# Page table in one transfer with the third weight block held back, and the samples' tile first in both output projections, in four column tiles

## What is computed

```python
def reference(x_prompt, x_sample, cache_kv_cmp, ..., page_table, w_in_even, ..., w_out_even, w_in_odd, ..., w_out_odd, ln_g, ln_b):
    for layer in range(DEPTH):                       # DEPTH = 2
        if layer % 2 == 0:                           # projection, convolution branch, sparse attention, output projection
            dp, a1, a2, a3, a4 = even_prompt(xp, w_in_even[j], ...)
            ds, b1, b2, b3, b4 = even_sample(xs, cache_kv_cmp[j], ..., page_table, w_in_even[j], ...)
        else:                                        # projection, pooling mixer, output projection
            dp, a5 = pool_mixer(xp, buf0, 0, w_in_odd[j], ...)
            ds, b5 = pool_mixer(xs, state_pool[j], past_len, w_in_odd[j], ...)
        ...
        xp = layer_norm(DEEPNORM_ALPHA * xp + dp, ln_g[layer], ln_b[layer])
        xs = layer_norm(DEEPNORM_ALPHA * xs + ds, ln_g[layer], ln_b[layer])
```

## Time and profile before

| | us |
|---|---|
| runs, median (lowest to highest) of 3 | 1087.09 (1086.37 to 1089.18) |
| the profiled execution, span | 1087.4 |
| PE busy | 1034.4 (95%) |
| DVE busy | 757.0 (70%) |
| ACT busy | 371.3 (34%) |
| POOL busy | 368.9 (34%) |

### The profile page before, as it was taken

How to read it: one execution, slowest core, us unless ns; L and a number is a source line. 1 busy time by engine, 2 the same in 40 slices (tenths; PEclk the granted TensorE clock), 3 DMA queues, 4 the chain that set the end, 5 groups by cost and what they waited for, 6 DMA issues and landing times.

```text
span 1087.4 us, 19270 instructions
## 1 busy us (share of the span) xinstructions
PE 1034.4 (95%) x7749; PEld 882.3 (81%) x7749; DVE 757.0 (70%) x1399; ACT 371.3 (34%) x784; POOL 368.9 (34%) x385
## 2 busy tenths in 40 slices
PE   6999999999999989989899999999999999999997
PEld 6888999999999955656555666787999999998875
DVE  3677889999899978877577755757545710267755
ACT  3211111212222657868566864201112211353000
POOL 3544530000110497866685652300122311318000
PEclk9999999999999999989999999999999999999998
DMA  8654322143312034130773058521231121042321
GB/s 239 219 169 175 116 100 59 39 178 102 113 40 44 1 112 134 40 118 2 229 239 117 2 203 223 156 83 63 78 97 39 39 58 46 1 155 78 136 82 63
DMA packets 85889, 113.75 MB, mean 105 GB/s; under 512 B 21952, under 2 KB 67144, under 8 KB 85727
## 3 DMA queue, kind: packets, MB, share of 16 engines
q1 hardware_dynamic: 71849, 69.51, 21.4%
q0 software_dynamic: 11776, 41.95, 11.5%
q10 hardware_dynamic: 2182, 1.16, 0.4%
HBM read 100.91 MB, written 16.64 MB: 108 GB/s over the span
## 4 chain that ended last, share of the span: by engine, by line
PE 78%; DVE 8%; DMA 4%; issue 3%; POOL 3%; ACT 2%; another core or an unknown queue 1%; SPq 1%; DVEq 0%; POOLq 0%; ACTq 0%
PE PS L786 23%; PE PS L2200 16%; PE PS L1968 13%; PE PS L1295 5%; PE PS L1425 5%; PE PS L1313 4%; PE PS L768 3%; PE PS L1992 2%; DMA WRAW<-in_w_in_even 2%; PE PS L1981 1%; DMA WOR<-in_w_out_even 1%; DVE ACC L608 1%; PE PS L2180 1%; DVE PT L1483 1%
## 5 line engine op out<-in xcount | busy, mean ns | idle before, releaser
L655 DVE SCALAR_TENSOR_TENSOR Y<-U,SM,Y 128x1024 f32<-128x1024 f32 x120 | 150.2, 1313 | 0.4
L786 PE MATMUL PS<-XH,WH 128*128 128x352 f32 x600 | 136.3, 331 | 0.0
L786 PE MATMUL PS<-XL,WH 128*128 128x352 f32 x600 | 133.7, 327 | 0.0
L786 PE MATMUL PS<-XH,WL 128*128 128x352 f32 x600 | 132.8, 325 | 0.0
L2307 POOL TENSOR_TENSOR WL<-WRAW,WH 128x1024 fp32r<-128x1024 f32 x14 | 37.5, 2675 | 208.7 <-ACT WH L2252 208.7
L608 DVE SCALAR_TENSOR_TENSOR ACC<-PS,SM,ACC 128x508 f32<-128x508 f32 x124 | 86.9, 742 | 25.1 <-PE PS L768 21.7
L786 PEld LDWEIGHTS PS<-XH,WH 128*128 128x128 f32 x600 | 101.2, 189 | 1.2
L786 PEld LDWEIGHTS PS<-XH,WL 128*128 128x128 f32 x600 | 101.6, 189 | 0.0
L786 PEld LDWEIGHTS PS<-XL,WH 128*128 128x128 f32 x600 | 101.4, 189 | 0.0
L2200 PE MATMUL PS<-XH,WH 128*128 128x352 f32 x360 | 77.2, 323 | 0.0
L2200 PE MATMUL PS<-XH,WL 128*128 128x352 f32 x360 | 77.1, 323 | 0.0
(11 more groups left out here) (364 smaller groups left out, 2009.6 us busy)
## 6 DMA issues: line engine op xcount, KB each, us to landing
WRAW<-in_w_in_even SPq DMA_DIRECT2D x16, 512.0 KB
WRAW<-in_w_in_odd SPq DMA_DIRECT2D x16, 512.0 KB, 4.0
TM<-in_state_win_kv SPq DMA_DIRECT2D x12, 512.0 KB
XIN<-in_x_prompt SPq DMA_DIRECT2D x8, 512.0 KB, 13.6
WRAW<-in_w_in_even SPq DMA_DIRECT2D x16, 256.0 KB
XR<-in_x_prompt SPq DMA_DIRECT2D x8, 512.0 KB, 3.6
layer_out<-R SPq DMA_DIRECT2D x8, 512.0 KB, 2.7
XR<-layer_out SPq DMA_DIRECT2D x8, 512.0 KB, 3.4
```

The lines of the kernel that those rows point to most:

```text
L655: v.scalar_tensor_tensor(dst, src, CWT[:, i, t:t + 1], dst, ALU.mult, ALU.add).then_inc(s_cv, 1)
L786: ins = pe.matmul(PS[0:mcols, 3 * slot + c, 0:CH], w[:, slot, kk, 0:mcols], x[:, kk, c * CH:(c + 1) * CH], start=(kk == 0 and n == 0), sto ...
```

## The change

In words, first at the start of the kernel:

- POOL loads the page table by one transfer, 8 rows of 16 numbers. DVE copies it eight times over into PTX, PE turns that into 128 partitions, and DVE makes the row numbers behind four tiles' low parts instead of six. PE's small transposes wait for these numbers.
- SP waits until weight block 1 has landed before it issues block 2.
- POOL makes the low part of block 0 in two halves, with a semaphore each. PE runs the first four weight rows behind tile 3, and tile 4 after them.

Then in both output projections:

- `TILES` begins with the samples' tile. The first parts are those of positions 1, 2 and 3; the samples' tile follows, then the rest. Banks, semaphore counts and, in layer 0, the points at which finished tiles are turned move with it.
- The samples' tile is computed in plain fp32 from the raw weights, with XS = XH + XL made by DVE: four weight blocks at a time in four column tiles, so that four partial sums lie in four groups of 32 partitions. DVE adds them.
- In layer 0 all eight raw blocks have a buffer of their own. SP loads blocks 6 and 7 directly behind 4 and 5, then the first two blocks of layer 1, and only behind the samples' matmuls GB and the pool state. ACT converts those two blocks of layer 1 after the first two square roots.

```diff
@@ sp_program @@
             sp.dma_start(STC[:, :, :], state_conv[0].rearrange("(a b) t c -> (b t) a c", a=2)).then_inc(s_stc, 16)
+            sp.wait_ge(s_raw[1], raw_need[1])
             for m in range(2, NM + 1):
@@ pool_program @@
-            for r in range(8):
-                po.dma_start(idx[r::8, 0:8], page_table.rearrange("b n -> n b")).then_inc(s_pt, 16)
+            po.dma_start(idx[0:DB, 0:NPG], page_table).then_inc(s_pt, 16)
...
-            low(po, 0)
-            po.wait_ge(s_idx, 1)
+            po.wait_ge(s_wh, 1)
+            for kks, sem in ((slice(0, 4), s_const), (slice(4, KT), s_wl)):
+                po.tensor_tensor(WL[:, 0, kks, :], WRAW[:, 0, kks, :], WH[:, 0, kks, :].bitcast(F32), ALU.subtract)\
+                    .then_inc(sem, 1)
+            po.wait_ge(s_idx, 3)
@@ dve_program @@
-            for tt in range(6):
+            v.wait_ge(s_pt, 16)
+            v.tensor_copy(PTX[:, :].rearrange("b (n r) -> b n r", r=8),
+                          idx[0:DB, 0:NPG].unsqueeze(2).to_broadcast([DB, NPG, 8])).then_inc(s_idx, 1)
+            for tt in range(4):
                 low_x(tt)
-            v.wait_ge(s_pt, 16 * 8)
-            link(v.tensor_copy(idxf[:, 0:8], idx[:, 0:8]))
+            v.wait_ge(s_idx, 2)
+            link(v.tensor_copy(idxf[:, 0:8], PS[:, 7, 0:8]))
...
-            for tt in range(6, NTT):
+            for tt in range(4, NTT):
@@ pe_program @@
             def turn_small():
                 pe.wait_ge(s_rows, 16 * 6)
+                pe.wait_ge(s_idx, 3)
...
-            for tt in range(5):
+            for tt in range(4):
                 turn_x(tt)
+                if tt == 1:
+                    pe.wait_ge(s_idx, 1)
+                    pe.transpose(PS[:, 7, 0:DB], PTX[:, :], ident[0:DB, 0:DB]).then_inc(s_idx, 1)
             first(0, range(4))
+            turn_x(4)
             turn_x(5)
@@ output projections @@
-                    pe_out_part(pe, 0, ev[1], range(FIRST_KK))
+                    pe_out_part(pe, 0, ev[1] + 1, range(FIRST_KK))
...
-        TILES = (0, 1, 2, 3, 4, 5, 8, 6, 7)
+        XS = [at(f"XS{i}", [P, KT, NSAMP], F32, o) for i, o in enumerate((200672, 181216))]
+
+        TILES = (8, 0, 1, 2, 3, 4, 5, 6, 7)
+        TURN_AFTER = {2: (0,), 4: (1, 2), 5: (3,), 6: (4,), 7: (5, 6)}
+        HIGH_BEFORE = {2: (0,), 4: (1, 2), 5: (3,), 6: (4,), 8: (5, 6)}
+        LOW_BEFORE = {3: (0,), 5: (1, 2), 6: (3,), 7: (4,), 8: (5, 6)}
@@ sp_out_loads, layer 0 @@
                 for kk in range(4, KT):
-                    if kk >= 6:
-                        wait_wol(sp, 0, kk - 4)
-                    else:
-                        wait_out(sp, 0, "woh", kk - 3)
+                    wait_out(sp, 0, "woh", kk - 3)
+                    if kk == KT - 1:
+                        sp.wait_ge(s_done_attn, 1)
...
-                    if kk == 5:
-                        sp.wait_ge(s_done_attn, 1)
-                        for i in range(2):
-                            wait_wol(sp, 0, i)
-                        for r, t in enumerate((ln_g, ln_b)):
-                            sp.dma_start(GB[:, r, :], t[0].partition_broadcast(P)).then_inc(s["gb"], 16)
@@ dve_out_samples instead of pool_out_samples @@
+        def dve_out_samples(v, layer):
+            v.wait_ge(*((s_ml, KT) if layer else (s_ol, 1)))
+            v.tensor_tensor(XS[layer][:, :, :], XHf[:, :, SEQ:T], XLf[:, :, SEQ:T], ALU.add).then_inc(OUT["xs"], 1)
@@ pe_out_samples @@
+            wait_out(pe, layer, "xs", 1)
+            for i in range(4):
+                wait_out(pe, layer, f"wor{i}", 16 if layer else 48)
+                if layer:
+                    pe.wait_ge(OUT[f"worb{i}"], 16)
+            for k0 in range(0, KT, 4):
+                for hf in range(2):
+                    for j in range(4):
+                        ins = pe.matmul(PS[NSAMP * j:NSAMP * (j + 1), b0 + hf, :], XS[layer][:, k0 + j, :],
+                                        raw_out(layer, k0 + j)[:, hf * 512:hf * 512 + 512],
+                                        start=(k0 == 0), stop=(k0 == KT - 4))
@@ dve_out @@
                     if TILES[tt] == SAMPLES:
-                        link(ins)
-                        ins = v.tensor_tensor(r, r, flat(PS[n:2 * n, b0:b0 + 2, :]), ALU.add)
+                        for j in range(1, 4):
+                            link(ins)
+                            ins = v.tensor_tensor(r, r, flat(PS[n * j:n * (j + 1), b0:b0 + 2, :]), ALU.add)
@@ sp_mixer @@
-            sp.dma_start(STP[:, :], state_pool[0].rearrange("b t c -> (b t) c")).then_inc(s_stp, 16)
             load_w2(sp, 0)
             load_w2(sp, 1)
+            for i in range(2):
+                wait_wol(sp, 0, i)
+            wait_out(sp, 0, "y", 1)
+            for r, t in enumerate((ln_g, ln_b)):
+                sp.dma_start(GB[:, r, :], t[0].partition_broadcast(P)).then_inc(OUT["gb"], 16)
+            sp.dma_start(STP[:, :], state_pool[0].rearrange("b t c -> (b t) c")).then_inc(s_stp, 16)
             sp_out_tiles(sp, 0)
```

More of the change, by code:

```diff
@@ L1787, in act_join @@
             act.wait_ge(s_done_attn, 1)
-            for tt in range(NTT):
-                act.activation(XH[:, 4:8, tok(tt)], BG[:, :, tok(tt)], ACT.Copy).then_inc(s_oh, 1)
+            for tile in TILES:
+                act.activation(XH[:, 4:8, tok(tile)], BG[:, :, tok(tile)], ACT.Copy).then_inc(s_oh, 1)
             act.wait_ge(s_ol, NTT)
@@ L1793, in dve_join @@
         def dve_join(v):
-            def low(tt):
+            for tt, tile in enumerate(TILES):
                 v.wait_ge(s_oh, tt + 1)
-                v.tensor_tensor(XL[:, 4:8, tok(tt)], BG[:, :, tok(tt)], XHf[:, 4:8, tok(tt)], ALU.subtract).then_inc(s_ol, 1)
-            for tt in range(NTT):
-                low(tt)
+                v.tensor_tensor(XL[:, 4:8, tok(tile)], BG[:, :, tok(tile)], XHf[:, 4:8, tok(tile)], ALU.subtract).then_inc(s_ol, 1)
+                if tt == 0:
+                    dve_out_samples(v, 0)
             dve_out_weight(v, 5)
@@ L1846, in rows @@
             def rows():
-                for tt in range(2):
-                    sp.dma_start(XR[layer][0:ntok(tt), tt, :], RES_IN[layer](tt)).then_inc(s[f"xr{tt}"], 16)
+                for tt, tile in enumerate(TILES[0:2]):
+                    sp.dma_start(XR[layer][0:ntok(tile), tt, :], RES_IN[layer](tile)).then_inc(s[f"xr{tt}"], 16)
                 for r, t in enumerate((ln_g, ln_b)):
@@ L2013, in pe_out @@
             if layer:
[L2014 removed]
+                part(1, range(FIRST_KK))
                 pe.wait_ge(s_ge, KT - 1)
[L2016 removed]
+                part(2, range(FIRST_KK))
                 pe.wait_ge(s_ge, KT)
[L2018 removed]
+                part(3, range(FIRST_KK))
             else:
                 pe.wait_ge(s_done_attn, 1)
[L2021 removed]
+                part(3, range(FIRST_KK))
             for tt in range(NTT):
@@ L2029, in pe_out @@
                 else:
-                    part(tt, range(FIRST_KK if tt < FIRST_TILES else 0, KT)).then_inc(s["y"], 1)
-                if layer == 0 and tt >= 2:
-                    if tt == 3:
-                        wait_out(pe, 0, "res", 3)
-                    turn(tt - 2)
+                    part(tt, range(FIRST_KK if tt <= FIRST_TILES else 0, KT)).then_inc(s["y"], 1)
+                for turned_tile in TURN_AFTER.get(tt, ()) if layer == 0 else ():
+                    if turned_tile == 1:
+                        wait_out(pe, 0, "res", 4)
+                    turn(turned_tile)
             if layer == 0:
@@ L2060, in dve_out @@
                 r, st = R[layer][0:n, tt % 3, :], BST[0:n, tt % 2, :]
-                if layer == 0 and tt >= 3:
-                    low(tt - 3)
+                for turned_tile in LOW_BEFORE.get(tt, ()) if layer == 0 else ():
+                    low(turned_tile)
                 wait_out(v, layer, "y", tt + 1)
+                if layer and tt == 0:
+                    wait_wol(v, 1, 4)
                 wait_out(v, layer, f"xr{tt % 2}", 16 * (tt // 2 + 1))
@@ L2103, in dve_out, with act_out @@
                 v.sem_inc(s_ev2, 2)
-                for tt in range(NTT - 3, NTT):
+                for tt in range(NTT - 2, NTT):
                     low(tt)
-        def act_out(act, layer):
+        def act_out(act, layer, next_weights=None):
             s = OUT
@@ L2120, in act_out @@
                 st = BST[0:ntok(TILES[tt]), tt % 2, 14:15]
-                if layer == 0 and tt >= 2:
-                    high(tt - 2)
+                for turned_tile in HIGH_BEFORE.get(tt, ()) if layer == 0 else ():
+                    high(turned_tile)
                 wait_out(act, layer, "var", tt + 1)
                 act.activation(st, st, ACT.Sqrt).then_inc(s["std"], 1)
+                if layer == 0 and tt < 2:
+                    next_weights(tt)
             if layer == 0:
```

55 lines of the change are left out of this document (20 added, 35 removed).

## The result

| | kernel before | changed kernel |
|---|---|---|
| median of the runs, same chip | 1087.68 us (1086.37 to 1089.18, 4 runs) | 1080.90 us (1075.91 to 1082.72, 4 runs) |
| ratio, 95% interval | | 0.9938 [0.9918, 0.9957] |
| the profiled execution: span, time | 1087.4, 1089.18 us | 1074.1, 1075.91 us |

The changed kernel is faster by 6.8 us; 13.3 were forecast, and the median lies 0.9 us above the range. The two traces differ by exactly the forecast, 1087.4 - 1074.1 = 13.3. That is a trap. The trace of after is the shortest of its four executions, 5.0 us under their median, and the trace of before the longest of its four, 1.5 us above.

The account below looks back on a forecast made before the run. TensorE (PE) was taken as the bound, holding 78% of the chain of waits. Start 4.9 + layer 0 5.2 + layer 1 3.2 = 13.3 us off 1087.4 gave 1074.1, stated as 1074.0 us; range 1071.0 to 1080.0.

Parts of the forecast that it names:

- The page table: Start: one transfer instead of eight fills the slow stretch from 6 to 13 us, every tile behind it 3.6 us earlier.
- Block 1 and the gap: Start: with block 2 held back, block 1 lands near 23 us; ScalarE's wait and PE's gap before line 816 go, 0.81 us.
- The reorder at the start: Start: tile 4 behind four weight rows lets matmuls start a tile earlier; taken as 0.5 us, at most 1.8.
- Packing: Samples' tile, both output projections: four column tiles side by side take 4.1 us, gaining 3.25 and 3.2 us.
- fourfold speed: Rival, samples' tile: column tiles run at full fourfold speed, 2.7 us a tile, total 1071.3 us; chance 0.06.
- in series: Rival, samples' tile: the four column tiles don't overlap, 16 us a tile instead of 4.1, total 1097.9 us; chance 0.03.
- Layer 0: Output projection of layer 0: faster samples' tile plus removed PE stall, 3.25 + 1.9 = 5.2 us, bounds 1.2 and 6.6.
- my second term: Output projection of layer 0: raw blocks 6 and 7 come earlier, so PE's stall for block 6's low part goes, 1.9 us.
- Layer 1: Output projection of layer 1: samples' tile first and computed faster, no wait, 0.7 us of room; gain 3.2 us.
- the start gains more: Rival, start: the reorder brings its whole 1.8 us and some of the gap before 15.13 goes, total 1072 us; chance 0.08.
- the hole stays: Rival, start: the slow transfer stretch is not the page table's; little but 0.8 us gained there, total 1078.2 us; chance 0.18.
- A new wait: Rival, layer 0: GB or raw block 7 comes late and costs PE 2 to 4 us, total 1077 us; chance 0.13.

Follow-up runs that it names:

- The mend: Changed kernel with ScalarE converting weight block 1 behind input tile 8 and, in layer 1, copying the samples' columns of GT instead of VectorE's sum: 1076.16 us, 0.9879.

## Why the prediction was wrong, step by step

**The page table: right.** 3.6 us forecast; alone it was worth 4.2 (2.3 to 5.1 by its interval), 3.7 by the first transpose against the first trace of before. The 0.7 us that I had estimated from a packet price are refuted: 1,024 single elements held the other transfers at 188 GB/s instead of 392 for 7 us. The Trainium skill, *DMA: Bandwidth & Descriptors*, section Bandwidth, has 64 packets in some 0.67 us, 10.5 ns each, but does not say that this is the price on each engine, as I had read it; counted over all engines together, the same figure would give an estimated 10.8 us.

**Block 1 and the gap: the step that failed.** It said that block 1 would land near 23 us, that ScalarE's wait and PE's gap of 0.81 would go, and that the gathers "may take back a part". Block 1 was converted at 25.3 to 27.5 us. The gathers had been at 25.57 in the trace of before, behind most of block 1's way; ready earlier by 7.5 us, they took 86.5% of the transfer time just when block 1 needed it. I priced the removed transfers and not the ones that would move into their place. The gap grew to 2.0 to 4.4 us. I had not counted at all that the granted clock would fall behind it, another 1.6 to 2.7 us in three traces of four. Forecast for the start 4.9; measured by the first transpose 1.5 (37.5, the mean of three old starts, less 36.0), and 1.4 in the time of the start alone. In the same means, PE reached the gap 4.9 us earlier (31.7, now 26.8; the forecast's tiles and reorder made 4.1); the longer gap took back 1.9 and the fall of the clock 1.4.

**The reorder at the start: small, as forecast.** 0.5 us forecast. The trace with the page table alone reaches the gap at 28.56 - 1.49 = 27.07 us, those of the changed kernel at 26.8 on average: some 0.3 us.

**New wait of VectorE for the table: right.** It landed 7.7 us after the start (forecast 7.6) and nobody waited for it.

**Packing: right, a little too dear.** 3.62 us against 4.1: sixteen in 3.62 are 0.91 us for four. By an estimated 0.67 us for one matmul of full width (from the 352 columns of the earlier trace rows) that is a speedup of 4 x 0.67 / 0.91 = 2.9. The fourfold of *TensorEngine Tiling (Array Packing)* (the Trainium skill, Theoretical Speedup) was not reached; the rivals "fourfold speed" and "in series" fall. The latter's 16 us a tile was at odds with my own bound of 10.7 for sixteen in series.

**Layer 0: 5.2 forecast, 5.0 in the pair, 3.1 to 5.0 over all traces.** The new stage is 98.97 to 99.00 us in all eleven traces that have it. The old one is 104.0 and 103.5 in the traces of before, and 102.1 in the three kernels that have the new start, or the new table alone, and the old output. There ScalarE has blocks 6 and 7 in time and PE has no stall. Both traces of before have one, of 1.34 and 1.10 us:

```profile
684.64 0.73 PE L1968 MATMUL PS<-WOH,XH 128*128 128x512 f32 x2 [1.10 <-POOL WOL L1938]
```

So the 1.9 us of my second term are a gain over the kernel before, but not one that the output part adds on top of the new start: the two gains can't simply be summed. Three traces don't tell whether the new start or chance takes the stall away. ScalarE in the kernel with the start part alone, against the earlier trace rows:

```profile
677.28 1.06 ACT L1932 ACTIVATE WOH<-WOR 128x1024 fp32r<-128x1024 f32 x1 [5.05 <-DMA WOR<-in_w_out_even]
679.76 1.06 ACT L1932 ACTIVATE WOH<-WOR 128x1024 fp32r<-128x1024 f32 x1 [1.42 <-DMA WOR<-in_w_out_even]
```

Its first output matmul is at 663.75, as in the trace of before, and its block 7 is converted 4.1 us earlier. Why these loads are faster there was not tried. Moving GB behind the samples' matmuls brought no wait, as said.

**Layer 1: 3.2 forecast, 2.2 measured.** The step "the sum adds 0.4, 0.7 us of room; a slip costs its own length" named the place. The size was off: 2.5 us instead of 0.4, beside POOL. The mend gave 1.2 back.

**Sum and reference.** "No more than 0.3 lies between" the profiled execution and the median was wrong. I compared a span with a time. Each run here takes 1.8 us more than its span, so the profiled execution of before, 1087.4, is the run of 1089.18, 1.5 us above the median. The attention alone differs by up to 5 us between executions of the same code (283.1 and 288.4 in two of after's traces), and it hid the error: in the first pair it gave by chance 2.5 us, about what the start (1.5) and layer 1 (1.0) had fallen short of the forecast. That the two traces differ by 13.3 is luck. With the terms as measured, 1.5 + 3.1 to 5.0 + 2.2 = 6.8 to 8.7 us; the medians gave 6.8 and 7.1. Where up to 1.9 us more are lost stays open: the attention is 284.4 us on average in the three traces with the old start and 285.7 in the thirteen with the new table, a difference that its scatter of 5 us doesn't let me call shown. Of the rivals, "the start gains more" and "the hole stays" fall by the traces. "A new wait" came true, but in the start and in layer 1, not in the place where I put it.

## What to carry to other kernels

In an early stage that is limited by transfers, what a removed transfer brings depends on what then comes into its place: list the transfers that become ready earlier and ask which needed one they run beside. An in-order engine that waits for a late block should have nothing behind it that a third engine needs soon; moving one conversion behind two input tiles was worth 6 us in the medians, on two chips, nearly as much as the whole change (4.4 us at the first compress transpose, in one trace of each). And a sum made from one pair of traces needs a second pair: compare stage by stage, and trust the stages that come out the same in all.

## What the runs showed of the hardware that was not expected

- In the start PE's granted clock went from 1.00 to 0.50 behind idle gaps of 2.53, 2.62, 3.09, 3.13, 4.39 and 5.66 us, and stayed at 1.00 in the ten traces whose gap was 0 to 1.99 us. The fall cost 1.4 to 2.7 us that the gap doesn't show: from the transposes of STC to the first compress transpose PE took 6.13 to 7.40 us instead of some 4.7. In the trace with 28 filler transposes in the gap the clock stayed at 1.00.
- 1,024 elements of 4 bytes, 2.1% of the engines' time by their own packets, halved the rate of all other transfers for 7 us (188 against 392 to 394 GB/s).
- A sum of 128x256 elements on VectorE took 0.43 us with POOL idle and 2.49 beside POOL's 128x1024 subtraction.
- Sixteen fp32 matmuls of 32 columns by 512, four side by side and accumulating in two banks, took 3.57 to 3.64 us in the traces read.
